# A decoder step on one core: the dt tables inside the first scan, layer-norm sums on VectorE, and one head's top-16 moved to the second pass

## The reference, cut to what matters

```
proj = x @ w_in                              # split into z, xBC, dt_raw, uv, gates
xBC  = silu(causal_conv(xBC));  dt = softplus(dt_raw + dt_bias);  A = -exp(a_log)
acum = cumsum(dt * A) in chunks of 128 tokens
y    = chunked scan: decay(acum) * (C B^T) @ (x * dt)  +  C @ state * exp(acum)
y_a  = rmsnorm(y * silu(z));   y_b = u * (W_s @ layer_norm(v) + b_s),  u, v = gelu(uv)
h    = layer_norm(ALPHA * x + (gate_a * (y_a @ wa) + gate_b * (y_b @ wb)) @ w_out)
# PEER: 8 heads, each: scores of two halves against 128 keys, top-16 of each half,
# top-16 of the 256 sums, softmax gates; 16384 experts, rows of 2048 numbers
act  = gelu(h . u_tab[expert]) * gate;  out = layer_norm(ALPHA * h + sum(act * v_tab[expert]))
```

## Time and profile before

| | us |
|---|---|
| median of three runs | 5251.36 |
| lowest, highest | 5247.69, 5252.13 |
| the profiled execution's own time | 5255.51 |
| span of that execution | 5253.8 |
| PE busy | 4537.9 (86%) |
| DVE busy | 2763.0 (53%) |
| POOL busy | 2161.2 (41%) |
| ACT busy | 856.8 (16%) |
| mean granted PE clock | 0.944 |

### The profile page before, as it was taken

One profiled execution on the slowest core, in us unless ns is written; L12 is line 12 of the kernel. 1 busy time (PEld: TensorE's weight loads), 2 busy tenths in 40 slices (PEclk: granted clock), 3 DMA queues, 4 the chain that ended last, 5 costly groups with the idle time before them and its releaser, 6 DMA issues. The chain is left out here.

```text
span 5253.8 us, 48208 instructions
## 1 busy us (share of the span) xinstructions
PE 4537.9 (86%) x18584; PEld 3403.6 (65%) x18584; DVE 2763.0 (53%) x3678; ACT 856.8 (16%) x1941; POOL 2161.2 (41%) x1647
## 2 busy tenths in 40 slices
PE   7999989999999988888878799998857777887776
PEld 5887878888888777777757687887743332332222
DVE  2545431100000668988966756666777665364445
ACT  2333321100000123333311110000111111110000
POOL 1766631000000244554532533332378885364442
PEclk8999999999999998999989899999878899899999
DMA  5565654444445379999989899999999999999998
GB/s 173 200 217 197 216 172 140 130 152 161 168 145 179 110 300 383 418 420 405 417 352 381 341 418 421 421 421 421 371 390 415 421 422 420 408 391 421 421 422 367
DMA packets 267292, 1674.46 MB, mean 319 GB/s; under 512 B 40032, under 2 KB 54944, under 8 KB 74016
## 3 DMA queue, kind: packets, MB, share of 16 engines
q0 software_dynamic: 160640, 1133.71, 52.7%
q1 hardware_dynamic: 101256, 536.48, 27.5%
q10 hardware_dynamic: 5168, 1.19, 0.1%
HBM read 1633.31 MB, written 37.89 MB: 318 GB/s over the span
## 5 line engine op out<-in xcount | busy, mean ns | idle before, releaser
L581 PE MATMUL psum<-rows_a,w_ring 128*128 128x264 f32 x6656 | 1509.4, 388 | 21.1 <-PEq L539 16.3
L581 PEld LDWEIGHTS psum<-rows_a,w_ring 128*128 128x128 f32 x6656 | 1270.4, 192 | 245.3 <-issue 27.4
L581 PE MATMUL psum<-x_and_spare,w_ring 128*128 128x256 f32 x5632 | 1253.7, 384 | 78.2 <-PEq L539 70.3
L581 PEld LDWEIGHTS psum<-x_and_spare,w_ring 128*128 128x128 f32 x5632 | 1082.4, 193 | 234.6 <-issue 81.6
L447 DVE SCALAR_TENSOR_TENSOR rows_a<-rows_a,h_tokens 128x2048 f32<-128x2048 f32 x388 | 888.8, 2293 | 404.9 <-DMA rows_a<-in_peer_u,expert 351.5
L392 POOL DMA_INDIRECT rows_a<-in_peer_u,expert x384 | 648.9, 1690 | 871.4 <-DVE rows_a L447 809.1
L392 POOL DMA_INDIRECT rows_a<-in_peer_v,expert x382 | 498.4, 1305 | 492.9 <-DVE h_tokens L470 217.4
L491 PE MATMUL psum<-rows_b,diags 128*128 128x512 f32 x1008 | 479.6, 625 | 193.4 <-ACT diags L481 146.0
L491 PE MATMUL psum<-rows_a,diags 128*128 128x512 f32 x1008 | 484.8, 630 | 153.6 <-ACT diags L481 108.1
L491 PEld LDWEIGHTS psum<-rows_b,diags 128*128 128x128 f32 x1008 | 193.0, 199 | 477.7 <-issue 296.5
L491 PEld LDWEIGHTS psum<-rows_a,diags 128*128 128x128 f32 x1008 | 194.8, 200 | 442.9 <-issue 295.4
(11 more groups left out here) (367 smaller groups left out, 3339.0 us busy)
## 6 DMA issues: line engine op xcount, KB each, us to landing
w_ring<-in_w_tiles SPq DMA_DIRECT2D x448, 1024.0 KB
rows_a<-in_state_ssm POOLq DMA_DIRECT2D x32, 512.0 KB, 6.0
out_ssm_sample<-rows_a POOLq DMA_DIRECT2D x32, 512.0 KB, 4.5
rows_a<-acum_rows_dram SPq DMA_DIRECT2D x16, 512.0 KB, 7.2
rows_a<-smp_bc_dram POOLq DMA_DIRECT2D x8, 1024.0 KB, 6.0
acts_by_token<-late SPq DMA_DIRECT2D x16, 512.0 KB, 7.5
branch_b<-acum_rows_dram SPq DMA_DIRECT2D x16, 512.0 KB, 8.9
rows_a<-in_xT SPq DMA_DIRECT2D x3, 2048.0 KB, 13.4
```

The costliest lines, as they stand in the source:

```text
L581: last = pe.matmul(o, w[:, k * P:(k + 1) * P], x[:, k, :], start=start and k == 0, stop=stop and k == KB - 1)
```

## The change

**Tables.** `tables` no longer opens a block. It takes its temporaries from `h_tokens` and returns functions that the first pass's `ssd` calls between its own instructions: `projections` ahead of the first weight tile, `totals` behind it, `turn_rows` behind tile 1, `spread` behind tile 2 on PE; `rates`, `decays`, `rows_and_decay` on ACT; `steps`, `fill`, `fill_samples` on DVE; `load` and `keep_rows` on SP; `constants` on POOL ahead of its state loads.

**Layer norm of the first pass.** For v and h `ln_add` sums the 16 blocks on DVE as they come, and one matmul (`ln_spread`) sums over partitions. For v `ln_fold` does the same with the squares; the squares of h stay with `ln_var`. The second pass keeps the matmuls.

**Head 7 of blocks 0 and 1.** The first pass selects heads 0 to 6. The scores of head 7 are copied by ACT to the end of `late`, and the second pass's scan selects them, one block at a time, in groups 2 and 4: `choose` on DVE before the expert steps of c = 1, `exps` on ACT at c = 2, `numbers` on POOL at c = 3, `inverse` and `shares` at c = 5 and 7. Its `Selection` is `lean` (it reuses parts of its own buffers). The counts of `head_done` and `gate_done` follow.

```diff
@@ first_pass
-            self.tables(xs, late)
-            self.clear_sems()
+            self.make = self.tables(xs, late)
             self.smp = Samples(self, cut, sb)
@@ tables: the same instructions, now in functions
+        cut = self.region(flat(self.htok[:]))
+        wdt = cut(KB, NH)
...
+        return dict(load=load, keep_rows=keep_rows, constants=constants, projections=projections, totals=totals,
+                    turn_rows=turn_rows, spread=spread, rates=rates, decays=decays, rows_and_decay=rows_and_decay,
+                    steps=steps, fill=fill, fill_samples=fill_samples)
@@ ssd, SP
+                if ps.i == 0:
+                    make["load"](sp)
...
+                        if ps.i == 0 and g == 0 and t == 1:
+                            make["keep_rows"](sp)
@@ ssd, PE
+                else:
+                    make["projections"](pe)
                 project(0, 0)
+                if ps.i == 0:
+                    make["totals"](pe)
                 for g in range(G):
                     project(g, 1)
                     if g > 0:
                         rms(g - 1)
+                    elif ps.i == 0:
+                        make["turn_rows"](pe)
                     project(g, 2)
+                    if ps.i == 0 and g == 0:
+                        make["spread"](pe)
@@ ssd, DVE, the second pass's expert steps
                 def expert(g, c):
+                    if ex and c == 1 and g in units:
...
+                        top.choose(o, dve, b, [kept[:, side, P * b:P * (b + 1)] for side in range(2)], ranked, b + 1,
+                                   picked)
@@ ssd, POOL
+                            if c == 3 and g in units:
+                                b = units[g]
+                                pool.wait_ge(picked, b + 1)
+                                o(top.numbers(o, pool, b))
...
+                            for s in self.steps(ps, "ssd", g, c):
+                                ex.rows(pool, s)
                 if ps.smp:
+                    make["constants"](pool)
@@ layer norm
+    def ln_add(self, dve, o, total, v, k, s):
+        dve.wait_ge(s["in"], k + 1)
+        if k == 1:
+            o(dve.tensor_tensor(total[:], v[:, 0, :], v[:, 1, :], ALU.add))
+        elif k > 1:
+            o(dve.tensor_tensor(total[:], total[:], v[:, k, :], ALU.add))
...
+    def ln_fold(self, dve, o, square, s):
+        for c in range(1, 4):
+            dve.wait_ge(s["square"], c + 1)
+            o(dve.tensor_tensor(square[:, 0:4, :], square[:, 0:4, :], square[:, 4 * c:4 * c + 4, :], ALU.add))
+        o(dve.tensor_tensor(square[:, 0:2, :], square[:, 0:2, :], square[:, 2:4, :], ALU.add))
+        dve.tensor_tensor(square[:, 0, :], square[:, 0, :], square[:, 1, :], ALU.add).then_inc(s["folded"], 1)
+    def ln_spread(self, pe, ps, bank, total, ready, done):
+        pe.wait_ge(ready, 1)
+        pe.matmul(self.bank[bank][:, 0:ps.n], self.onesD[:], total, start=True, stop=True).then_inc(done, 1)
@@ sgu, PE (back has the first two edits)
-                    if m > 0:
+                    if m > 0 and not ps.smp:
                         self.ln_mean(pe, ps, v, m - 1, ln)
-                self.ln_mean(pe, ps, v, FT - 1, ln)
+                if ps.smp:
+                    self.ln_spread(pe, ps, 2, root[:], ln["added"], ln["mean"])
...
-                self.ln_var(pe, ps, yb, ln)
+                if ps.smp:
+                    self.ln_spread(pe, ps, 3, yb[:, 0, :], ln["folded"], ln["summed"])
@@ back, POOL, ACT and DVE of the first pass
-                    elif m % 2 == 1:
+                    elif m % 2 == 1 and p < PH - 1:
                         heads(p)
...
+                        if m >= FT - 2:
+                            act.copy(kept[:, m - FT + 2, :], sc[m % 2][:, 0:ps.np])
...
-                for m in range(0 if pick else FT):
+                for m in range(0 if pick else FT - 2):
```

More of the change, by code:

```diff
@@ new lines, in projections @@
+        def projections(pe):
+            pe.wait_ge(x_in, 48)
+            for k in range(KB):
+                last = pe.matmul(dth[0][0:NH, 0:NA], wdt[:, k, :], xs[:, k, :],
+                                 start=(k == 0), stop=(k == KB - 1))
+            last.then_inc(head_done, 1)
+            pe.wait_ge(xb_in, 16)
+            for k in range(KB):
+                last = pe.matmul(dth[1][0:NH, 0:TP - n0], wdt[:, k, :], xb[:, k, :],
+                                 start=(k == 0), stop=(k == KB - 1))
+            last.then_inc(head_done, 1)
+            pe.wait_ge(made, 1)
+            pe.wait_ge(head_copied, 3)
+            for c in range(CH):
+                last = pe.transpose(dtp[:, c * NH:(c + 1) * NH], dts[:, c * P:(c + 1) * P],
+                                    self.ident[0:NH, 0:NH])
+            last.then_inc(proj_done, 1)
@@ new lines, in totals, with turn_rows @@
+        def totals(pe):
+            pe.wait_ge(dtA_ready, 1)
+            pe.matmul(ac[:, 0:NC], self.triu[:], dtA[:, 0:NC], start=True, stop=True)
+            pe.matmul(ac[:, NC:2 * NC], self.ones[:], dtA[:, 0:NC],
+                      start=True, stop=True).then_inc(sums_done, 1)
+        def turn_rows(pe):
+            pe.wait_ge(acum_ready, 1)
+            for k in range(2):
+                last = pe.transpose(self.bank[6][:, k * P:(k + 1) * P], v["n"][:, k * P:(k + 1) * P],
+                                    self.ident[:])
+            last.then_inc(rows_turned, 1)
@@ new lines, in spread, with rates @@
+        def spread(pe):
+            pe.wait_ge(diag_ready, 1)
+            for s in range(2):
+                last = pe.matmul(bcs[s][:, 0:NS * NH], self.ones[0:NH, :],
+                                 diag[:, s].rearrange("p b h -> p (b h)"), start=True, stop=True)
+            last.then_inc(spread_done, 1)
+        def rates(act):
+            act.wait_ge(in_sem, 16)
+            act.activation(arow[:, 0:NH], rows[:, NH:2 * NH], ACT.Exp)
+            act.activation(arow[:, NH:NH + 1], rows[:, 2 * NH + 1:2 * NH + 2],
+                           ACT.Exp).then_inc(rate_ready, 1)
+            act.wait_ge(head_done, 1)
+            act.copy(dts[:, 0:n0], dth[0][0:NH, 0:n0]).then_inc(head_copied, 1)
+            act.copy(dts[:, TP:T], dth[0][0:NH, n0:NA]).then_inc(head_copied, 1)
+            act.wait_ge(head_done, 2)
+            act.copy(dts[:, n0:TP], dth[1][0:NH, 0:TP - n0]).then_inc(head_copied, 1)
+            act.wait_ge(neg_ready, 1)
+            act.activation(v["u"][:], v["n"][:], ACT.Exp).then_inc(u_ready, 1)
+            act.wait_ge(w_ready, 1)
+            act.activation(v["l"][:], v["w"][:], ACT.Ln).then_inc(ln_ready, 1)
+            act.wait_ge(par_in, 32)
@@ L1276, in _ @@
                     conv(g, 2)
+                    if ps.i == 0 and g == 0:
+                        make["fill_samples"](dve, o)
                     if g > 0:
@@ L1747, in _ @@
                             x_ready=(lambda k: (merge_done, k + 1)) if m == 0 else None)
[L1748 removed]
+                    if m > 0 and not ps.smp:
                         self.ln_mean(pe, ps, h, m - 1, ln)
[L1750 removed]
+                if ps.smp:
+                    self.ln_spread(pe, ps, 2, root[:], ln["added"], ln["mean"])
+                else:
+                    self.ln_mean(pe, ps, h, FT - 1, ln)
                 self.ln_var(pe, ps, merged, ln)
```

357 lines of the change are left out of this document (178 added, 179 removed).

## The result

The changed kernel takes 5223.44 us (median of 5 runs, 5217.87 to 5224.56) against 5251.12 us before. The ratio is 0.9946, 95% interval 0.9932 to 0.996: about 28 us faster, where 31 were forecast (5220.6 us). The profiled execution's span is 5221.3 us against 5253.8. It shows 32.5 us, some 5 more than the medians do; the experiments come back to that.

The account below looks back on a forecast made before the run. PE was taken to bound the first pass and DVE the second pass's scan. The terms -22.5 - 18.6 - 6.7 + 17 = -30.8 us gave a median of 5220.6 us, range 5204 to 5238.

Parts of the forecast that it names:

- Term 1: Start of the first pass: tables made inside the scan bring the fourth weight tile earlier; -22.5 us, from -18 to -25.5.
- d: Delay of x's landing at the start, from POOL's state loads issued beside it; 0 to 6 us, taken as 3.
- Term 2: Layer norms of the first pass, `sgu` and `back`: PE matmuls replaced by DVE sums; -18.6 us, from -16.5 to -20.
- Term 3: End of the first pass: without head 7 POOL ends earlier and SP is next late; -6.7 us, -5 to -8.
- Term 4: Two selections in the second scan, where DVE sets the pace: 8.5 us a unit, +17 in all.
- B: Second scan: selections cost the upper bound, POOL's pause uncovered or DVE held by POOL; +31, 5234.6 us; chance 0.17.
- E: Second scan: late gathers make DVE run dry, 27 us a unit; 5257.6 us; chance 0.04.
- C: Second scan: selections are free, the DMA engines being the true bound; 5203.6 us; chance 0.10.
- D: Start: x lands late and the clock falls in PE's gaps, gain 12 instead of 22.5; 5231 us; chance 0.07.

Follow-up runs that it names:

- e4: Changed kernel with the tables again a stage of their own ahead of the first scan; 5247.0 us, ratio 0.9991 to the kernel before.
- e6: Changed kernel with POOL's first sample-state loads (1.2 MB) waiting until x has landed; 5219.7 us, ratio 0.9949 to the kernel before.
- e11: Changed kernel with the sums and squares of v in the first pass's `sgu` on PE again; 5231.84 us, ratio 0.9971 to the kernel before.
- e8: Changed kernel with the sums of h in the first pass's `back` on PE again; 5230.14 us, ratio 0.9965 to the kernel before.
- e1: Changed kernel with the last head selected in the first pass again; 5216.0 us, ratio 0.9929 to the kernel before.
- e7: Changed kernel with the store of `x_rows` issued ahead of the last query weights; 5223.59 us, ratio 0.9949 to the kernel before.
- e5: Changed kernel with PE's rms matmuls of the first scan issued one weight tile later; 5189.88 us, ratio 0.9892 to the kernel before.
- e3: Changed kernel without POOL's computation of the expert numbers in the two selections; 5216.79 us, ratio 0.9936 to the kernel before.
- e2: Changed kernel with the same two selections in group 0 of the second scan; 5205.38 us, ratio 0.9924 to the kernel before.
- e9: Changed kernel with the four edits of e2, e5, e6 and e7 together; 5163.98 us, ratio 0.9828 to the kernel before.
- e10: e9 plus three extra PE matmuls, result unused, in the gap before the mean in the first pass's `back`; 5168.9 us, ratio 0.9837 to the kernel before.

## Why the prediction was right, and where not

The forecast was 2.8 us too low in the median, with the sign and the main mechanisms right. That the sum came so near is partly luck: in the profile 9.7 us that nobody forecast (first scan 6.6, behind the second scan 3.1) stand against 8.1 us that it hoped for and did not get (the second scan 3.6, `back` 3.0, ahead of `w_out` 1.2, `sgu` 0.3). Step by step:

**Term 1 (22.5 us): right.** The trace has 22.6, e4 has 23.6. d was taken as 3; x came 4.45 us late, but the first projection was 1.5 us shorter. e6 shows that d was the states' loads and could be had back. The DMA engines were called not full in that burst; the row had them at a share of 0.95.

**Term 2 (18.6): right in `sgu`, mis-sized in `back` by one profile.** `sgu` gained 12.7 in the trace and 13.3 in e11. In `back` the step "w_out waits 1.79 us for weights, so 0.9 us are only waited away" was near (3.07 us now). What the sum did not have is the squares of `back`, which took 7.39 us before and 9.07 after. I had taken them as unchanged, and e8 shows that they are no fixed number: the same instructions took 10.3 us there. Since the stretch took 135.1 to 137.3 us with the sums on DVE and 137.9 and 143.7 with them on PE, what `back` gained lies anywhere from 0.6 to 8.6 us.

**Term 3 (6.7): right,** 6.6 in the trace and 6.7 in e1. SP was named as next late, and it is. But I took its path as fixed. The longest piece of it, the wait for the store of `x_rows`, stood between the two issues of the earlier trace rows, and e7 takes 5.6 us off it by one move.

**Term 4 (+17): right in size, with one wrong reason.** The profile has 20.5 us between first and last rms, and by it the sum is 3.5 us short. But e5 to e8 and e11 have the same selections in the same groups and took 16.8 to 17.8 us over before and e1: 8.4 to 8.9 a selection, forecast 8.5. Most of the 3.5 us is the longer wait for PE that the profile of the changed kernel has from group 4 on. The price of POOL's part, "1 to 2 us a unit", came out at 1.6 to 2.0 (e3). Its reason did not: the prediction had the numbers hold back gathers, and no wait for gathered rows shows in groups 2 and 4. They took DVE time instead, 1.5 and 1.8 us. The pause itself was 13.75 us and not the 5.9 of the earlier trace rows, a row in which DVE stood still for most of the time.
I had weighed there what the Trainium skill (SBUF — State Buffer, "Who interferes with whom") says of DVE instructions with two SBUF inputs and GpSimd instructions. The trace agrees that they hold each other up, the second to issue waiting for the first, and it shows this on both engines. POOL's addition of 32 elements, issued at 2085.74 us, 0.2 us behind a dot, took 2.19 us. DVE's three convolution products, the first issued at 2082.58 while POOL's product ran until 2083.77, took 2.93 us instead of 1.52. What was wrong is my working, that by the rule all 5.9 us would come on DVE: most of the holding up fell on POOL.
The rest, about 6.9 us a selection, is near the 6.6 of the row of the tail.

**The rivals.** B (15.5 us a unit) and E (27) are out: 9.7 and 11.2 us were measured, with 9.1 to 9.2 for group 4 in e5 to e8 and e11. E's own price of 27 us gives 5257.6, which by the prediction's bound of 5261.9 would not even have been slower. C (free) is false in groups 2 and 4 and nearly true in group 0 (e2). D is out.

**What the prediction did not have.** The profile's 32.5 us against the medians' 28 is mostly the first scan: 6.6 us there that the change hardly made. The prediction has PE as the bound there, without a pause between tiles, and takes no note of the wait before the rms. It was the largest wait of the first pass that an experiment removed: e5 took 33.6 us off by hiding it (28 by the ratios).

The change as it stands thus carries one part that loses. Undone (e1) it is 7.4 us faster, by the profiles' stretches 10 to 14; moved to group 0 (e2) 18 us by the medians, 12 by the ratios. With that move, the later rms and the two queue moves the kernel takes 5164.0 us, 1.7% below the kernel before.

## What to carry to other kernels

Work moved off a critical engine must be priced at its new place: the same two selections cost 17 to 20 us where DVE was already busy about 90% of a group and about 3 us where it was busy 65%. Before a sum is made from one profile, look whether a stretch that the change does not touch repeats; the first scan's differed by up to 12 us between kernels that are the same there, which is nearly half of this change's effect. And where a wait recurs once a group, see what else PE could do first: one tile's reordering gave as much as the three parts of this change together.

## What the runs showed of the hardware

POOL's elementwise instructions beside DVE's dots were held up by about one dot each (2.2 us for 32 elements). DVE's dots were not held up in group 2 (2.28 to 2.31 us); in group 4 one took 2.69 us. DVE's product of 1024 columns took 3.22 us beside POOL's product of two SBUF operands, issued 0.23 us before it, and 1.23 us where POOL issued gathers. Whichever of the two was issued second paid.

Once PE did not idle before the rms, its eight matmuls took 1.89 us and each group the same time to 0.01 us, in e5 and in e9. With 4.08 us of idleness ahead they took 3.78 us in the group at 379 us, and the granted clock of that stretch was 0.50, the lower of the two levels (1.2 GHz); behind a wait of 3.91 us in the group at 134 us they took 1.99 us, at 1.00. And a gap of 1.2 us filled with matmuls (e10) left the clock of the next ones as it was, so an idle gap just ahead is not the whole of what sets it.
